# Hand-overs between sub-layers: three of the second half's four additions of squares and cross products move from VectorE to GpSimd

## The reference, cut to what matters

```python
def run_trunk(x, ...):                      # x: 512 prompt rows and 32 sample rows, width 1024, fp32
    f1 = swiglu(rmsnorm(x, ffn1_pre_g), ...)       # hidden width 2816
    x = x + 0.5 * rmsnorm(f1, ffn1_post_g)
    y = token_mixing(rmsnorm(x, mix_pre_g), ...)   # conv, conv31, RWKV-7, pooling; then w_out
    x = x + rmsnorm(y, mix_post_g)
    f2 = swiglu(rmsnorm(x, ffn2_pre_g), ...)
    x = x + 0.5 * rmsnorm(f2, ffn2_post_g)
```

## Time and profile before

| what | us |
|---|---|
| median of 3 runs | 1122.28 (1121.89 to 1124.95) |
| time of the profiled execution | 1119.76 |
| its span | 1118.0 |
| TensorE busy | 1071.3 (96%) |
| VectorE busy | 799.1 (71%) |
| ScalarE busy | 462.0 (41%) |
| GpSimd busy | 282.1 (25%) |

### The profile page before, as it was taken

One profiled execution on the slowest core, in us unless ns is written; L12 is line 12 of the kernel. 1 busy time (PEld: TensorE's weight loads), 2 busy tenths in 40 slices (PEclk: granted clock), 3 DMA queues, 4 the chain that ended last, 5 costly groups with the idle time before them and its releaser, 6 DMA issues. The chain is left out here.

```text
span 1118.0 us, 23301 instructions
## 1 busy us (share of the span) xinstructions
PE 1071.3 (96%) x9146; PEld 1048.0 (94%) x9146; DVE 799.1 (71%) x1224; ACT 462.0 (41%) x776; POOL 282.1 (25%) x217
## 2 busy tenths in 40 slices
PE   6999999999999989999889999999999999999995
PEld 6999999999999988999777789899999999999995
DVE  5657689536985876888879627867577984399746
ACT  6432455415654433511234433433235552256520
POOL 0220666034540000120233000004135531265201
PEclk9999999999999989999879989989999999999998
DMA  6332223322324121233701002113232324223212
GB/s 213 101 94 94 86 103 113 102 87 77 113 75 132 41 88 57 64 75 95 50 2 40 2 1 97 57 35 98 67 122 79 110 77 149 76 76 113 93 58 81
DMA packets 35400, 92.04 MB, mean 82 GB/s; under 512 B 10368, under 2 KB 12928, under 8 KB 35328
## 3 DMA queue, kind: packets, MB, share of 16 engines
q1 hardware_dynamic: 34320, 88.78, 25.9%
q10 hardware_dynamic: 1008, 2.27, 0.6%
HBM read 87.76 MB, written 3.28 MB: 81 GB/s over the span
## 5 line engine op out<-in xcount | busy, mean ns | idle before, releaser
L315 PE MATMUL ps<-xh,wh 128*128 128x272 f32 x816 | 194.4, 301 | 18.7 <-DVE xl L499 8.6
L824 PE MATMUL ps<-seven,wh 128*128 128x272 f32 x1024 | 195.1, 287 | 0.0
L315 PE MATMUL ps<-xh,wl 128*128 128x272 f32 x816 | 190.4, 296 | 0.0
L315 PE MATMUL ps<-xl,wh 128*128 128x272 f32 x816 | 190.4, 296 | 0.0
L298 DVE TENSOR_TENSOR wl<-raw,wh 128x1024 fp32r<-128x1024 f32 (+1 forms) x99 | 118.3, 1197 | 80.2 <-ACT wh L293 79.9
L315 PEld LDWEIGHTS ps<-xh,wh 128*128 128x128 f32 x816 | 140.3, 196 | 22.0 <-DVE wl L298 12.1
L824 PEld LDWEIGHTS ps<-seven,wh 128*128 128x128 f32 x1024 | 159.8, 188 | 0.0
L315 PE MATMUL ps<-hh,wh 128*128 128x272 f32 x704 | 156.2, 288 | 0.0
L315 PE MATMUL ps<-hh,wl 128*128 128x272 f32 x704 | 155.3, 288 | 0.0
L315 PE MATMUL ps<-hl,wh 128*128 128x272 f32 x704 | 155.1, 287 | 0.0
L293 ACT ACTIVATE wh<-raw 128x1024 fp32r<-128x1024 f32 (+1 forms) x99 | 100.0, 1018 | 126.0 <-PE ps L315 58.6
(11 more groups left out here) (350 smaller groups left out, 1915.4 us busy)
## 6 DMA issues: line engine op xcount, KB each, us to landing
raw<-in_w_gu SPq DMA_DIRECT2D x88, 512.0 KB, 3.8
raw<-in_w_d SPq DMA_DIRECT2D x32, 512.0 KB, 3.6
raw<-in_w_in SPq DMA_DIRECT2D x19, 512.0 KB, 3.6
raw<-in_w_d SPq DMA_DIRECT2D x16, 384.0 KB, 3.0
raw<-in_w_out SPq DMA_DIRECT2D x8, 512.0 KB, 3.6
out_y<-x SPq DMA_DIRECT2D x16, 136.0 KB
x<-in_x ACTq DMA_DIRECT2D x4, 272.0 KB, 5.5
x<-in_x SPq DMA_DIRECT2D x4, 272.0 KB, 6.5
```

Source lines behind the costliest of these rows:

```text
L315: last = pe.matmul(out[:, n], left[:, s, j], right[:, j, n * H:n * H + H], start=first and opens and j == order[0], stop=final and closes ...
L824: last = pe.matmul(out, left[:, j], right[:, j], start=m in (0, 1, 3) and j == 0 and left is hi and right is high, stop=j == 3 and left is ...
```

## The change

In both hand-overs the additions L484 of the second half for d = 4, 5 and 6 are taken out of VectorE's order and given to GpSimd, in a new function that calls the same helper; the additions for d = 7 stay with VectorE. VectorE's cross products for d = 6 and 7 of the second half write into the `sq3` place that d = 4 and 5 used, and so wait for GpSimd's addition of two rows before.

```diff
         def half_cross_dve(dve, n, h, d):
             dve.wait_ge(S("f_half"), place_of(n, h, d) + 1)
+            if h and d > 5:
+                dve.wait_ge(S("h_add"), 6 * (n // 2) + 3 * h + d - 5)
...
+        def hand_over_pool(pool, n):
+            for d in range(4, 7):
+                half_squares_dve(pool, n, 1, d)
+
         def hand_over_dve(dve, n, u, leave_half):
...
             leave_half(1, 4)
             half_cross_dve(dve, n, 1, 4)
             split_lo(dve, u, 0, 0, KD)
-            half_squares_dve(dve, n, 1, 4)
             rows_dve(dve, n, 0, 0, 1)
...
             half_rec_dve(dve, n, 0, 1)
             split_lo(dve, u, 0, 1, KD)
             rows_dve(dve, n, 0, 2, 3)
-            half_squares_dve(dve, n, 1, 5)
             split_lo(dve, u, 0, 2, KD)
             leave_half(1, 6)
             half_cross_dve(dve, n, 1, 6)
             rows_dve(dve, n, 0, 3, 4)
             leave_half(1, 7)
             half_cross_dve(dve, n, 1, 7)
-            half_squares_dve(dve, n, 1, 6)
             half_squares_dve(dve, n, 1, 7)
...
         @block.gpsimd
         def _(pool):
             ffn_pool(pool, 0, 0)
+            hand_over_pool(pool, 1)
             mixer_pool(pool)
+            hand_over_pool(pool, 3)
             ffn_pool(pool, 1, FFN2)
             final_pool(pool)
```

## The result

The changed kernel is slower: over 20 runs each, 1123.22 us (1117.38 to 1130.17) against 1115.95 us (1110.0 to 1127.49); the ratio is 1.0053, 95% interval 1.0034 to 1.0073, that is 5.9 us (3.8 to 8.1); the two medians lie 7.3 us apart. Note the 1115.95: the 1122.28 before the prediction was the median of three runs, and 17 more brought it down by 6 us. The profiled execution of the changed kernel took 1122.36 us, its span is 1120.6 us.

What follows compares the result with a forecast made beforehand. TensorE, busy 96% of the span, was taken as the bound, with VectorE's time in the hand-overs on its path. Holds less relief of 6.8 us plus 0.9 for the clock gave 7.7, hence 1130.0 us, range 1124.0 to 1134.0.

Steps and rivals of the forecast that it cites:

- the mechanism: In both hand-overs, VectorE instructions with two SBUF inputs and GpSimd's additions exclude each other; one waits for the other's end.
- I add the 7.7 to the median: The forecast loss of 7.7 us was put on the median of the kernel before, giving 1130.0 us.
- Removed additions: Relief on VectorE: d = 4 worth 0, then at most 0.92 us; d = 5 0.92 in both hand-overs; d = 6 0.
- D: Time of one moved GpSimd addition of 816 elements, holding VectorE's next instruction: 1.9 us, ends 1.71 and 2.34.
- d = 6, the mis-sized term: In each hand-over one of L507, L522, L512 is held, making L487 and TensorE's sum 1.9 us later.
- whoever waits goes first: Between VectorE and GpSimd, the one already waiting gets the next turn, even with VectorE's next instruction right behind.
- A sign that didn't come: TensorE's wait for L487 was to rise by about 2 us in each hand-over.
- The clock: TensorE's longer waits bring some 2 us more work at half rate: 0.9 us, bounds 0 to 3.0.
- New waits, `mixer_pool`, the second `ffn_pool`: Cross products' waits for GpSimd cost nothing; both pools start some 20 us after GpSimd's last addition: 0.
- Relief without exclusion: Rival: no exclusion for these shapes, so the third-place L298 comes earlier in both hand-overs; −2.0 us, 1120.3; 9%.
- Holds that don't hurt: Rival: GpSimd gets turns only when VectorE reads PSUM or is idle; about one hold a hand-over stays; +3, 1125.3; 8%.
- Longer half rate by one stretch of 3.3 us: Rival: TensorE's half rate lasts one such stretch longer in both hand-overs; 6.8 + 3.0 = 9.8 us, 1132.1; 10%.

Runs made afterwards that it cites:

- after_again: The changed kernel run again unaltered for a second profile; ratio to the kernel before 1.0049 (1.0023 to 1.0076).
- tiny: Changed kernel with GpSimd's six additions cut to one column (3 elements a partition instead of 816); ratio to the kernel before 1.0014.
- probe_add: Kernel before plus three GpSimd additions of 816 elements that nobody uses, in the first hand-over alone; ratio to the kernel before 1.0034.
- probe_set: Kernel before plus three pairs of GpSimd memsets of 1088 elements, reading nothing, in the first hand-over alone; ratio to the kernel before 0.9995.
- pieces: Changed kernel with each GpSimd addition of 816 elements cut in three of 272; ratio to the kernel before 1.0079.

## Why the prediction was right and wrong

**Direction and size.** I forecast +7.7 us (0.69%); measured are 5.9 (0.53%, 0.34 to 0.73%), or 7.3 by the two medians. The sign, the mechanism and the lost relief held. That the size came so near is in part luck: the holds were smaller than forecast and the clock cost more. The absolute time, 1130.0 with a range from 1124.0 to 1134.0, missed 1123.22.

**The step that failed first: "I add the 7.7 to the median".** The three runs shown gave 1122.28, twenty give 1115.95. On that base the same sum is 1123.7. Even twenty runs don't fix the base: beside the experiments the kernel before has medians of 1118.15 to 1119.13 (17 to 35 runs), and the changed kernel had 1125.1 (after_again), which lies inside the range. The runs of this kernel spread over more than 1%, which my range didn't take in: with three runs from 1121.9 to 1125.0 I took the base as known to some 3 us. Most of the spread goes with the clock. Over the 20 runs of the changed kernel the span falls as the mean granted clock rises (correlation -0.92): 1115.6 us at 0.973, 1126.9 at 0.960. Why one run has more time at half rate than the next stays open. A clock 0.013 lower means 2 x 0.013 x 1120 = 29 us more at half rate, and 11.3 us more time, 0.39 us a us, near the 4.4 us for 10.2 that the prediction took from the earlier trace rows.

**Removed additions.** Right, by tiny: 0 for d = 4 in the first hand-over, 0.1 in the second beyond the wait for `rbp`, 0.92 for d = 5, 0 for d = 6.

**D and the holds.** D = 1.9 was a little high: the additions took 1.78 us when VectorE was off, and a hold costs VectorE 1.67. The estimate of 1.79 by the Trainium skill's GPSIMD Engine Reference, Performance versus the Vector engine, was nearer. So d = 5 is +0.75 (forecast 0.98), d = 4 in the second hand-over +0.77 (0.98), d = 4 in the first 0 (0.02).

**d = 6, the mis-sized term.** "One of L507, L522, L512 waits D", 1.9 us in each hand-over. It was 1.7 where L512 was held and 0.1 where the turn went to it and the cross product was held, behind which there is slack for ScalarE. I had read from L861 that whoever waits goes first; at this place it is not settled by that. In L487's place the sum is 4.1 us in the first profile (0.88 + 3.24) and 5.7 in the second (2.48 + 3.25), for 6.8. Nor does all of it reach TensorE's later work: in after_again's first hand-over L487 is 2.48 us later, but L2082 behind it only 0.95 (434.54 us, with L405 at 382.47, against 431.89 and 380.77). There TensorE ran at 0.53 from 394.3 to 401.1 us, ahead of L487, where it had time to spare, and for 6.8 us instead of 10.2 behind it.

**A sign that didn't come.** I expected TensorE's wait for L487 to grow by about 2 us in each hand-over. It went from 1.3 to 1.4 and from 1.33 to 1.0 us (after_again: 1.0 and 1.8). In the first profile's second hand-over TensorE was at half rate ahead of L487, took longer for the products there and so came later to the wait; L487 itself was 3.24 us late.

**The clock.** I gave 0.9 us. The mean clock is 0.9681 in the 35 runs of before beside after_again, 0.9663 in the changed kernel's 20 and 0.9655 in its further 12 (for the 20 of before it isn't on record): 4 to 6 us more at half rate, some 2 us. Larger than my value, inside its bounds, and it partly makes up for the smaller holds. A straight line through each kernel's runs gives at a clock of 0.968 some 1118.8 us for before and 1121.6 and 1122.0 for the changed kernel: by this estimate about 3 us of the loss stand at an equal clock, and the rest goes with the clock.

**New waits, `mixer_pool`, the second `ffn_pool`.** 0 each, as forecast: nobody waits for one of GpSimd's six additions in the profile of the changed kernel.

**The rivals.** Relief without exclusion is out by probe_add. Holds that don't hurt came true in part, for d = 6. Longer half rate by one stretch of 3.3 us came true in the second hand-over of both profiles (some 17 us in all against some 14, the pieces just behind the hand-over counted), in the first hand-over only in after_again (13.6 against 10.2).

## What to carry to other kernels

An elementwise addition handed to GpSimd doesn't run beside a VectorE instruction with two SBUF inputs. In this kernel (816 fp32 elements a partition) it took 1.7 us from VectorE and gave 0.9 us back, unless VectorE was idle, worked from PSUM or had time to spare for another engine there. A profile has to be read for what stands behind each removed row: of six removed additions two and a bit were worth anything. And where TensorE waits for 1 to 3 us in a dense kernel, look at the granted clock behind the wait; matmuls without use in the wait were worth more (0.6%) than any move between VectorE and GpSimd tried here. Where single runs differ by 1%, forecast the difference and not the absolute time, take the base from twenty runs or more of the same series, and read each time beside its mean clock.

## What the runs showed of the hardware that I had not expected

- The turn between a waiting GpSimd instruction and the VectorE instruction behind the running one isn't fixed: GpSimd arriving 0.14 us after the start of a 0.5 us VectorE row got the next turn in seven of ten cases. Behind the second L298 of 1.2 us, where it arrived over 0.5 us before the end, it got it each time (ten of ten, for d = 5).
- 26 matmuls without use in each hand-over took the mean clock from 0.968 to 0.9765 and 7 to 8 us off the time (0.62%).
- Stretches at half rate come at other places in other executions: at 710 us in the profile of before, at 384 us in that of probe_set (behind no wait), at 25 us in that of pieces. One execution's profile shows one draw.
